# Second mixer rearranged: q, k and V columns by head halves, softmaxes between the units of V, output units ahead of the last head norm, trigonometry in the prologue

## The reference

```
h = rmsnorm(x, norm_g)
q, k, v = jnp.split(h @ w_qkv, 3, axis=-1)
...
q = partial_rope(rmsnorm(q, q_g), positions)
k = partial_rope(rmsnorm(k, k_g), positions)
lam = exp(sum(lam_q1 * lam_k1)) - exp(sum(lam_q2 * lam_k2)) + lambda_init
p = softmax(q @ k^T * scale)        # per head and part c = 0, 1
a = p[:, :, 0] - lam * p[:, :, 1]
o = rmsnorm(a @ v, subln_g) * (1.0 - lambda_init)
x = x + o @ w_out
```

## Time and profile before

| | us |
|---|---|
| median of 3 runs | 1878.59 (1877.34 to 1879.49) |
| the profiled execution | 1878.4 |
| its span, first to last instruction | 1876.6 |

### The profile page before, as it was taken

One profiled execution on the slowest core, in us unless ns is written; L12 is line 12 of the kernel. 1 busy time (PEld: TensorE's weight loads), 2 busy tenths in 40 slices (PEclk: granted clock), 3 DMA queues, 4 the chain that ended last, 5 costly groups with the idle time before them and its releaser, 6 DMA issues.

```text
span 1876.6 us, 32956 instructions
## 1 busy us (share of the span) xinstructions
PE 1855.0 (99%) x11258; PEld 1559.6 (83%) x11258; DVE 1425.0 (76%) x2625; ACT 975.8 (52%) x1395; POOL 105.9 (6%) x71
## 2 busy tenths in 40 slices
PE   8999999999999999999999999999999999999999
PEld 6778888888888888888876688888888888888887
DVE  5575688988888888655588756889888888885555
ACT  5465555555545444444566655565455444444443
POOL 0000341000000000000000013510000000000000
PEclk9999999999999999999999999999999999999999
DMA  6445455555555555555553254555555555555555
GB/s 230 135 135 169 158 179 190 183 176 178 173 170 168 174 178 179 190 192 191 198 167 125 90 169 162 181 183 191 174 173 176 170 169 171 177 179 191 196 192 171
DMA packets 89488, 326.16 MB, mean 174 GB/s; under 512 B 10064, under 2 KB 10192, under 8 KB 89040
## 3 DMA queue, kind: packets, MB, share of 16 engines
q1 hardware_dynamic: 88848, 323.00, 53.0%
q10 hardware_dynamic: 576, 2.33, 0.3%
HBM read 324.24 MB, written 1.05 MB: 173 GB/s over the span
## 4 chain that ended last, share of the span: by engine, by line
PE 93%; DVE 4%; ACT 2%; issue 0%; DMA 0%; ACTq 0%; DVEq 0%
PE ps L1492 25%; PE ps L1490 14%; PE ps L1736 13%; PE ps L1738 12%; PE ps L1737 12%; PE ps L1489 4%; PE ps L1684 3%; PE ps L1508 2%; PE ps L1510 2%; PE ps L1509 2%; DVE wl L828 1%; PE ps L1665 1%; PE ps L1628 1%; ACT big L754 0%; DVE hT L837 0%
## 5 line engine op out<-in xcount | busy, mean ns | idle before, releaser
L828 DVE TENSOR_TENSOR wl<-raw,wh 128x1024 fp32r<-128x1024 f32 x569 | 696.5, 1227 | 162.0 <-ACT wh L468 153.3
L468 ACT ACTIVATE wh<-raw 128x1024 fp32r<-128x1024 f32 x609 | 641.6, 1055 | 317.0 <-PE ps L1738 165.0
L1492 PE MATMUL ps<-hT,wh 128*128 128x512 f32 x2072 | 739.2, 396 | 0.0
L1490 PE MATMUL ps<-hT,wl 128*128 128x256 f32 x2368 | 613.3, 279 | 0.0
L1490 PEld LDWEIGHTS ps<-hT,wl 128*128 128x128 f32 x2368 | 446.8, 189 | 25.0
L1492 PEld LDWEIGHTS ps<-hT,wh 128*128 128x128 f32 x2072 | 389.7, 188 | 78.8
L1736 PE MATMUL ps<-wh,hT 128*128 128x512 f32 x1024 | 402.2, 393 | 0.3 <-DVE big L812 0.2
L1738 PE MATMUL ps<-wh,hT 128*128 128x512 f32 x1024 | 399.3, 390 | 0.0
L1737 PE MATMUL ps<-wl,hT 128*128 128x512 f32 x1024 | 398.7, 389 | 0.0
L1738 PEld LDWEIGHTS ps<-wh,hT 128*128 128x128 f32 x1024 | 192.3, 188 | 40.2
L1736 PEld LDWEIGHTS ps<-wh,hT 128*128 128x128 f32 x1024 | 192.4, 188 | 39.6 <-issue 0.9
(11 more groups left out here) (225 smaller groups left out, 1347.2 us busy)
## 6 DMA issues: line engine op xcount, KB each, us to landing
raw<-stream SPq DMA_DIRECT2D x612, 512.0 KB, 3.4
big<-keys ACTq DMA_DIRECT2D x2, 1024.0 KB, 8.4
x<-x_in SPq DMA_DIRECT2D x1, 1024.0 KB, 5.4
out<-x SPq DMA_DIRECT2D x4, 256.0 KB, 2.1
sm<-small ACTq DMA_DIRECT2D x1, 228.5 KB, 5.6
pos_i<-positions ACTq DMA_DIRECT2D x1, 1.0 KB, 6.5
```

The source lines that it names most:

```text
L468: act.activation(wh[:, r, :], raw[:, r, :], ACT.Copy).then_inc(high_ready, 1)
L828: dve.tensor_tensor(wl[:, r, :], raw[:, r, :], wh[:, r, :].bitcast(F32), ALU.subtract).then_inc(made_low(unit), 1)
L1490: pe.matmul(near, w_l[:, kd, :], hTh[:, kd, :], start=False, stop=False)
L1492: i = pe.matmul(wide, w_h[:, kd, :], both, start=False, stop=(kd == KD - 1))
```

## The change

- **Block order.** The column blocks come as `QKV_BLOCKS` = 0, 2, 1, 3, 4, 5: q of heads 0 to 3, k of heads 0 to 3, then the other halves, then V. The host lays the weights out so.
- **Norms at once.** DVE norms a block in its own turn, and PE transposes it ahead of the next block but one (`qkt(0)`, `(1)`, `(2)` ahead of blocks 2, 3, 4), the last one after 15 of V's 32 chunks. A chunk is three matmuls of a unit.
- **POOL.** `on_pool` now takes the odd-numbered of the 24 qkv units too: POOL makes `low` of 12 of them (the first, third, and so on).
- **Softmax steps between V's chunks.** Step j stands ahead of chunk `STEP_AT[j]` = 12, 13, 14, 15, 17, ... 30. It holds scores j, the transposes of j - 3 and, from step 5 to 11, the product with V of j - 4 (step 5 has that of 0 too). The `keep_warm` of each step is gone. Heads 0 to 3 share bank 5 for their products, so the product of a new head waits until DVE has copied the head before (`o_got`), which DVE does in its steps 6, 8, 10 and 12. Products of heads 4 to 7 come after V's last chunk.
- **The end.** The first head norms and their transposes come between the last products, and the three first output units ahead of the norms of heads 4 to 7.
- **Trigonometry.** DVE works out the angles and the sums for lam ahead of the first norm of the kernel, right after a wait for the small inputs. ACT's sine and exponential, and lam, move to the query units of the first feed-forward network.

```diff
+QKV_BLOCKS = 0, 2, 1, 3, 4, 5
...
+        rope = sb("rope", [P, 2, NT, ROPE_HALF])
...
+        a_da = area(17664, 4, S)
+        aT_da = area(12288, 16, NT, P)
...
-        PAIR_BANK = {1: (2, 3, 2, 3), 4: (0, 1, 2, 3)}
-        OUT_BANKS = (0, 6), (4, 6)
+        PAIR_BANK = {1: (2, 3, 2, 3), 4: (0, 1, 4, 5)}
+        OUT_BANKS = (0, 6), (2, 0)
...
-        QKT_BEFORE = (3, 0), (4, 0), (5, 0), (5, 2)
+        QKT_BANKS = (0, 1), (2, 3), (0, 1), (6, 7)
+        QKT_LAST_AT = 15
+        STEP_AT = tuple(12 + 5 * j // 4 for j in range(16))
...
-            return any(0 <= unit - unit_of[f"u{l}"] < POOL_UNITS and unit % 2 == 1 for l in range(2))
+            return unit % 2 == 1 and (0 <= unit - unit_of["qkv"] < U_QKV or
+                                      any(0 <= unit - unit_of[f"u{l}"] < POOL_UNITS for l in range(2)))
+        def aT_bank(n):
+            return 4 if n < 13 else 4 + n % 2
...
+                if l == 1:
+                    pool.wait_ge(low_odd, unit_of["qkv"] // 2)
+                    for v in range(U_QKV):
+                        if on_pool(unit_of["qkv"] + v):
+                            low(unit_of["qkv"] + v)
...
+                    if l == 0 and u == 2:
+                        act.wait_ge(trig_step, 1)
+                        act.activation(rope[:], rope[:], ACT.Sin).then_inc(trig_step, 1)
+                    if l == 0 and u == 5:
+                        act.wait_ge(lam_ready, 1)
+                        act.activation(lam[:, 2:4], lam[:, 0:2], ACT.Exp).then_inc(lam_ready, 1)
...
-            act.wait_ge(trig_step, 1)
-            act.activation(trig[:, 6:8], trig[:, 4:6], ACT.Sin).then_inc(trig_step, 1)
-            act.wait_ge(lam_ready, 1)
-            act.activation(lam[:, 2:4], lam[:, 0:2], ACT.Exp).then_inc(lam_ready, 1)
...
+                if nb >= 1:
+                    qkt_got(nb - 1)
...
+            preload(ACT.Exp)
+            ahead(unit_of["qkv"] + 18)
...
+            for j in range(16):
+                if j == 3:
+                    qkt_got(3)
+                if j == 4:
+                    v_got(4)
+                    da_out(0)
+                ahead(unit_of["qkv"] + 16 + STEP_AT[j] // 4)
+                da_exp(j)
+                if j >= 4:
+                    da_out(j - 3)
+                if 7 <= j < 15:
+                    h, t = (j - 7) // 2, (j - 7) % 2
+                    head_squares(o_da, h, t, (o_got, h + 1), sq_o)
+            preload(ACT.Sqrt)
+            v_got(5)
+            head_std(0, 1)
...
+            ahead(unit_of["wo1"])
...
+            dve.wait_ge(loaded_small, 32)
+            chain(dve.tensor_copy(trig[:, 0, :, 0], pos_i[:]))
+            for k in range(ROPE_HALF):
+                i = dve.tensor_scalar(trig[:, 1, :, k], trig[:, 0, :, 0], float(ROPE_INV[k]), None, ALU.mult)
+            chain(i)
...
+            dve.tensor_scalar(rope[:], trig[:, 1:3], PI_SAFE, -PI_SAFE, ALU.min, ALU.max).then_inc(trig_step, 1)
+            lv = sm[:, SM_LAM:SM_LAM + 256].rearrange("p (a d) -> p a d", a=4)
+            chain(dve.tensor_tensor(sq[:, 0, 0:128].rearrange("p (a d) -> p a d", a=2), lv[:, 0:4:2, :],
+                                    lv[:, 1:4:2, :], ALU.mult))
+            dve.tensor_reduce(lam[:, 0:2], sq[:, 0, 0:128].rearrange("p (a d) -> p a d", a=2), AX, ALU.add
+                              ).then_inc(lam_ready, 1)
...
-            dve.wait_ge(loaded_small, 32)
...
-                if nb < 4:
-                    qk_mean(nb)
-                    ahead(unit_of["qkv"] + 4 * nb + 4)
-                if 1 <= nb <= 4:
-                    qk_norm(nb - 1, unit_of["qkv"] + 4 * nb + 5 if nb < 4 else None)
-            ahead(unit_of["qkv"] + U_QKV - 1)
+                cols = slice(QKV_BLOCKS[nb] * 512, (QKV_BLOCKS[nb] + 1) * 512)
+                dve.tensor_copy(QK[:, 0, cols], ps[:, 4 + 2 * (nb % 2), :]).then_inc(qkv_out_v, 1)
+                ahead(unit_of["qkv"] + 4 * nb + 4)
+                qk_mean(nb)
+                ahead(unit_of["qkv"] + 4 * nb + 5)
+                qk_norm(nb, unit_of["qkv"] + 4 * nb + 6)
...
-                if n >= 2:
-                    dve.wait_ge(aT_mm, n - 1)
...
+                if n >= 4:
...
+            def da_got(h):
+                dve.wait_ge(o_mm, h + 1)
+                dve.tensor_copy(o_da[:, :, h, :], ps[:, 5, 0:S].rearrange("p (t d) -> p t d", t=NT)).then_inc(o_got, 1)
+            def da_got_two(k):
+                dve.wait_ge(o_mm, 5 + k)
+                dve.tensor_copy(o_da[:, :, 4 + 2 * k:6 + 2 * k, :],
+                                ps[:, 6 + k, :].rearrange("p (h t d) -> p t h d", h=2, t=NT)).then_inc(o_got, 1)
...
-            for n in range(16 + 5):
-                if n < 16:
-                    da_max(n)
...
-                if 1 <= n < 17:
-                    da_sums(n - 1)
-                if 2 <= n < 18:
-                    da_difference(n - 2)
...
-                if n >= 5:
-                    da_got(n - 5)
...
+            for j in range(16):
+                if j == 4:
+                    v_got(4)
+                ahead(unit_of["qkv"] + 16 + STEP_AT[j] // 4)
+                da_max(j)
+                if j >= 1:
+                    da_sums(j - 1)
+                if j >= 2:
+                    da_difference(j - 2)
+                if j in (6, 8, 10, 12):
+                    da_got((j - 6) // 2)
...
+            da_sums(15)
+            v_got(5)
+            da_difference(14)
+            da_difference(15)
+            head_scale(0, 1)
+            for pair in range(2):
+                head_norm(o_da, pair)
...
+            for pair in range(2):
+                heads_transposed(4, pair, da_scale)
+            for k in range(2):
+                da_got_two(k)
+            ahead(unit_of["wo1"] + 1)
...
-            for nb in range(6):
-                for q in range(4):
-                    if (nb, q) in QKT_BEFORE:
-                        qkt(QKT_BEFORE.index((nb, q)))
-                    token_unit(unit_of["qkv"] + 4 * nb + q, q, lambda t: ps[:, 4 + 2 * (nb % 2) + t, :], qkv_mm,
-                               lambda t: qkv_bank(nb, t))
-            pe.wait_ge(qkv_out_v, 6)
-            pe.wait_ge(qkv_out_a, 6)
-            pe.wait_ge(qkt_out, 8)
...
-                keep_warm(2 * (n % 2), 1)
+                if n in (0, 8):
+                    pe.wait_ge(qkt_out, 6 if n == 0 else 8)
...
-                if n >= 2:
-                    pe.wait_ge(aT_out, n - 1)
+                if n == 0:
+                    pe.wait_ge(qkv_out_v, 5)
+                    pe.wait_ge(qkv_out_a, 5)
+                elif n == 13:
+                    pe.wait_ge(o_got, 4)
+                else:
+                    pe.wait_ge(aT_out, n if n < 13 else n - 1)
...
+                if h < 4:
+                    bank, at_ = 5, t * P
+                    if t == 0 and h >= 1:
+                        pe.wait_ge(o_got, h)
+                else:
+                    bank, at_ = 6 + (h - 4) // 2, (h % 2 * 2 + t) * P
+                    if n == 8:
+                        pe.wait_ge(qkv_out_v, 6)
+                        pe.wait_ge(qkv_out_a, 6)
...
-            for n in range(16 + 4):
-                if n < 16:
-                    da_scores(n)
-                if 3 <= n < 19:
-                    da_turn(n - 3)
-                if n >= 18:
-                    head_transposes(4, n - 18)
-                if n >= 4:
-                    da_values(n - 4)
-            out_projection(1, 4, ((aT_out, 16), (o_got, 16)))
+                if n in (1, 3, 5, 7, 11, 15):
+                    i.then_inc(o_mm, 1)
+            def da_step(j):
+                if j == 4:
+                    da_turn(0)
+                da_scores(j)
+                if j >= 4:
+                    da_turn(j - 3)
+                if j == 5:
+                    da_values(0)
+                if 5 <= j < 12:
+                    da_values(j - 4)
+            def v_chunk(at_):
+                if at_ in STEP_AT:
+                    da_step(STEP_AT.index(at_))
+                if at_ == QKT_LAST_AT:
+                    qkt(3)
+                if at_ == 16:
+                    pe.wait_ge(qkt_out, 8)
...
+            for nb in range(6):
+                if 2 <= nb < 5:
+                    qkt(nb - 2)
+                for q in range(4):
+                    token_unit(unit_of["qkv"] + 4 * nb + q, q, lambda t: ps[:, 4 + 2 * (nb % 2) + t, :], qkv_mm,
+                               lambda t: qkv_bank(nb, t),
+                               lambda t, k: v_chunk(16 * (nb - 4) + 4 * q + 2 * t + k) if nb >= 4 else None)
+            da_turn(13)
+            for n in range(8, 12):
+                da_values(n)
+            da_turn(14)
+            da_turn(15)
+            for pair in range(2):
+                head_transposes(4, pair)
+            for n in range(12, 16):
+                da_values(n)
+            out_projection(1, 4, ((pe_ready, 32), (hT_ready, 36)))
             ffn(1)
@@ -1868,7 +1944,7 @@
```

(2 more changed lines are left out.)

185 lines of the change are left out of this document (78 added, 107 removed).

## The result

The changed kernel takes 1905.11 us (median of 4 runs, 1904.04 to 1906.40) against 1878.74 of the kernel before: 1.0142 times, 95% interval 1.0124 to 1.0159. It is slower by 26.4 us. The forecast was 1885, range 1871 to 1892: the direction was right, the size was not, and the time lies outside the range.

A forecast was written before the change was run, and what follows sets the result against it. The prediction took PE, busy nearly all the span, to bound the kernel. To 1878.4 it added 2.1 for the mixer and 4.1 for the prologue: 1884.6, given as 1885 against the median, with 8 in 10 between 1871 and 1892.

The forecast's parts named there:

- the prologue: Kernel start: angle work delays DVE's first norm by 3.3 us, low clock adds 0.8; 4.1 in all.
- the norm ahead of the mixer: DVE's last two of four scalings wait for POOL's low: between 0 and 1.9 us, taken as 1.9.
- the waits at the q/k transposes: In the q and k blocks, PE waits for norms that POOL delays on DVE: 6.0 us taken.
- at the third scores: PE waits for the late last k block: 2.6 us in place of 0.7, so 1.9 more from POOL.
- what would show it: Trace signs listed for right or wrong, such as `var` at about 12.0 and no gap at the fifth unit.
- the sum of the changed mixer: Work, standing waits and POOL's part together: 112.4 us against 110.3, 2.1 slower, with the norm's 1.9 included.
- Waits that stand even if nothing else goes wrong: PE's mixer waits for copies of finished heads (4.8), at entry and at the end: together 9.5 us.
- The clock: After a long PE wait in the mixer the clock may fall, as once before at 1.6 us; 0.8 taken.
- V in pieces: Softmax steps changing places with V's matmuls cost a little each time: 0.8 us in all (0 to 1.6).
- the first turn: The first transposes, in step 4, wait for ACT's copies of q, k and V behind its exponentials: 1.3 us.
- the fourth: Rival: POOL always first, with two falls of the clock: 1892 us, up to 1895; chance 0.08.
- POOL's 10.6: POOL's low parts holding DVE up in the mixer: 6.0 + 1.9 + 0.8 + 1.9 = 10.6 us.

The follow-up runs named there:

- no_pool: The changed kernel with DVE making all low parts of the q, k and V units again and POOL none: 1900.7 us, 4.4 less.
- refill_late: The changed kernel with ACT and DVE preparing the next weight unit behind each softmax step's own work, not ahead of it: 1897.4 us, 7.7 less.
- warm_in_waits: The changed kernel with 16 and 12 warming matmuls ahead of PE's waits for the first and third q/k transposes: 1906.3 us.
- before_angles: The kernel before with only the angle work, lambda's sums, sine and exponential moved beside layer 0's query units: 1872.9 us, 4.6 less.
- before_pool: before_angles with POOL making the low parts of every second q, k and V unit: 1881.1 us, 8.2 more than before_angles.
- angles_late: The changed kernel with angle work and lambda's sums moved from the prologue to beside layer 0's query units: 1900.8 us, 4.3 less.

## Why the forecast missed

Two terms held in size and in mechanism: the prologue 3.66 (4.1) and the norm ahead of the mixer 1.79 (1.9). They rest on rows in which the same thing, or nearly the same, happened. The next two came near in size: the waits at the q/k transposes 7.7 (6.0) and at the third scores 2.76 (2.6). That is partly luck, since the forecast put 6.0 and 1.9 of them down to POOL holding DVE up, and in no_pool, with POOL out of it, 4.0 and 4.45 are still there. The signs named under "what would show it" came too: `var` at 12.03, no gap at the fifth unit, norm steps of over 3 us beside POOL, three gaps ahead of products with V (the third 3.74 and not 1.6). Only the wait at the second group was not there.

The step that failed is the sum of the changed mixer: 110.5 by the forecast (without the norm's 1.9), 131.55 measured, 21.0 more. The forecast had 92.3 of work, 17.4 of waits and 0.8 for the clock. Measured are 26.7 of waits (9.3 more), 9.4 for the clock (8.6 more) and 95.4 of work (3.1 more). In the forecast's own terms:

- **A wait that I did not write down, some 7.** "Waits that stand even if nothing else goes wrong" names copies of heads, entry and end, and not the preparation of the weight units that fall due among the steps (V's last and three of the output projection), which `ahead` puts in front of the step in ACT's and DVE's queues. I had looked at which engine has room, and not at what stands between the scores and their maximum. In the profile these are 2.36, 0.51 and 2.68 at the transposes and 2.1 of the 3.74; refill_late gives 7.7 back, with part of these waits still there and the waits and the clock at the third scores included.
- **The clock, 9.4 in place of 0.8.** I priced half a fall, by the earlier trace rows, for a mixer in which I had myself counted ten waits. Of those over 1.5 us five were followed by 3 to 6 us at 0.50. By the row that I used, the term had to be taken for several of them. Some of it costs nothing, though: in the q and k blocks DVE sets the pace (warm_in_waits).
- **V in pieces, 3.0 in place of 0.8.** This has a row now (0.87 against 0.68 for a chunk). My upper bound was 1.6.
- **The smaller ones.** The waits at the transposes were 1.7 longer, the rest of the steps' waits within 0.5 of their terms: 1.57 and 1.51 for the first two copies (1.6 each), 2.22 and 0.95 at the end (1.8 and 0.9), 0.46 at the first turn (1.3).

Of the rivals, the fourth came nearest ("POOL always first, with two falls of the clock", 1892), and it had the wrong reason for the rest. No rival was a mixer in which the spread itself costs. As to causes by experiment, from the changed kernel's 1905.1 down: POOL 4.4, refills 7.7, angles 4.3 (12.4 together), copies of heads 4.6, the spread 4.6. Of these the forecast had priced POOL (10.6), the angles (4.1) and the copies (4.8), and not the refills and the spread. The last 10.7 us down to before_angles lie mostly in the q and k blocks (7.5 in the traces), where PE waits for the last instruction of a norm that stands in its block's own turn. That is read from the traces; no run moved the norm back alone, so it isn't shown by itself.

POOL's 10.6 needs a word of its own. The mechanism is shown: DVE's instructions stand still beside POOL's, in the norm and in the blocks. The size was wrong for the changed kernel, where taking POOL's share away gives 4.4. The 8.2 of before_pool is nearer, but it belongs to a kernel whose norm stands a block later, so it doesn't check the sum. Once DVE is late for another reason, POOL's delay hides in part beside it, and POOL does spare DVE two `low` per block.

## What to carry to other kernels

Where two kinds of work are interleaved on one engine, write out what stands on the other engines between each result and its next use, the preparation of the interleaved work included; idle shares do not show it. A wait of the matrix engine can cost twice, once as idle and once as the low clock behind it (five of the nine long ones here), unless another engine sets the pace anyway. And before a large change, look whether its cheapest part does the job alone: here one block of angle work, moved to where DVE waits, gave 4.6 us, and all of the rest cost 28 (angles_late against before_angles).
